# First modulation row summed by VectorE, and the lagged output matrices formed piecewise during the first projection

## The chip, the cores and the metric

The kernel runs on one core of a Trainium2 chip. The time is the device time of one execution, in microseconds (us). The kernel before takes 1801.37 us, the median of 3 runs (1799.45 to 1803.9). The profile comes from one further execution of 1798.16 us, whose span from its first to its last instruction is 1796.2 us.

## The reference, cut to what matters

The program is a stack of eleven phases over 256 tokens of width 1024: attention with compressed keys (mla), an MLP, a state-space mixer (s5), an MLP, and then gated feed-forward blocks with a recurrent block and a second attention between them. Everything is float32. The change touches only the first phase and what is prepared in it for later ones:

```python
cs = jax.nn.silu(c)                                   # (1, 1024)
shift, scale, gate = jnp.split(cs @ mod_mix_w[0] + mod_mix_b[0], 3, axis=-1)
h = x * (1.0 + scale) + shift                         # input of the first mixer
z = h @ w_in                                          # 448 columns: the first projection
cq = rms_norm(z[..., :256]); ckv = rms_norm(z[..., 256:384]); k_pe = rope(z[..., 384:])
q, kv = cq @ w_qb, ckv @ w_kvb                        # then causal attention over 8 heads
...
# s5, two phases later: y = C x, with C given as c_re, c_im (64 groups of 16 x 64)
# the kernel steps two tokens at a time and so also needs C times the decay ("lagged" matrices)
```

`mod_mix_w[0]` is 1024 x 3072; its first third gives the shift, the second the scale. The remaining thirds of the first two modulations (gate, and the shift and scale of the MLP behind) are needed only after the attention.

## The kernel before, in words

Each engine has its own instruction queue, written out by hand, and waits on named counters. Weights are streamed in chunks: SyncE (SP) issues `line(c)`, which loads chunk c of 1 MB into one of five `raw` slots; ScalarE (ACT) rounds it to a high part in `hi(c)`; VectorE (DVE) forms the remainder in `lo(c)`; TensorE (PE) multiplies with three products a tile. `line(c)` waits until the chunk that held its slot has been used.

The start. SP issues eight transfers of 1 MB, n = 0 to 7 (L590), two row blocks of one third each: n = 0 to 3 are the shift, 4 to 7 the scale. They go into four buffers `m0`, so that n = 4 to 7 each wait until PE has used the piece four places ahead (`m0_used`). PE multiplies each piece with the broadcast `csB` (L1157). Behind n = 5 SP issues chunk 0 of w_in, behind n = 6 the input x, and after n = 7, without any wait, chunks 1 and 2, two norm rows, two modulation pieces (L492) and chunks 3 and 4. ACT meanwhile issues its own transfers: three short ones, `b_re` and `b_im` of s5 (L1659, each 128 partitions x 32 runs of 64 bytes, 4096 pieces) and 16 small ones for `c_re` and `c_im` (L1665, 128 runs of 256 bytes each). Only after the last of them does ACT form the rotation table (L1382), copy the transposed decay parameters (L1669), round chunk 0, and, once GpSimd (POOL) has reduced the angles (POOL from L2344, counter `s5p_pool` at 2), form their exponentials and sines. DVE waits for the same counter for a reciprocal (L2274) and then builds h (L2282, L2283). PE transposes h (L714) and projects it in four passes `z_pass`.

Between the first projection and the attention. DVE normalises and rotates z (L1977 to L1982), forms the remainders for PE, and then `output_lag`, six operations on 128 x 1024 that turn the output matrices into the lagged ones (L2035 to L2040). It stands behind four transposes of c by PE (`s5_turn`, L948) and four copies by ACT (`s5_matrix`). POOL waits for it (`s5_lag`), stores the result, forms the input matrices (L2390 to L2394) and clears `wide_row` (L2410); ACT waits for that clearing in step 1 of the attention (`same_step`, L1410).

The modulation pieces. A later third is summed by DVE from four pieces of 1 MB, `piece(n)`: two scalar_tensor_tensor operations on 128 x 1024 (L1829, L1830). SP loads them with `fetch(n)` (L492) into two buffers, so `fetch(n)` waits for `piece(n - 2)`. Pieces 0 and 1 stand ahead of the two rotations of q, pieces 2 to 9 at the end of steps 0 to 3, 5, 6, 8 and 9 of the attention, chunk remainders `lo(6)` and `lo(7)` in steps 4 and 7, and pieces 10 and 11 behind. In SP's queue, 13 loads of short vectors (`cols`, L532, element by element) stand between `fetch(7)` and `fetch(8)`.

A step i of the attention on DVE: scale and mask the scores of head i (L2070, L2071) and take their maxima (L2074), normalise head i - 1 (L2080 to L2082), then from step 3 on form the remainder `hlo` of the output of head i - 3 (L1720), and then the piece. PE starts the output projection when the last `hlo` is there.

## Time and profile before

| | |
|---|---|
| median of 3 runs | 1801.37 us |
| profiled execution | 1798.16 us, span 1796.2 us |
| busy in the span | PE 92%, DVE 63%, ACT 46%, POOL 8% |
| busy in the first 200 us | PE 153.01, DVE 127.31, ACT 74.40, POOL 50.99 us |
| chain that ended last | PE 70%, DVE 16%, ACT 5% of the span |
| mean granted TensorE clock | 0.959 |

The page shows PE full from about 200 us on. Everything that the change touches lies ahead of that, in a stretch where PE has gaps. There the chain of waits runs through other engines and through transfers, and the busy shares of the page say little. The queues q1 and q10 are those of the transfers that SP and ACT issue; a "packet" is one contiguous piece of a transfer.

### The profile page before, as it was taken

The numbers are of one execution on the slowest core, as the hardware profiler recorded it, in microseconds if no ns is written. First come the engines' busy times: TensorE is split into PE (matmuls) and PEld (weight loads), VectorE is DVE, ScalarE is ACT, GpSimd is POOL, SyncE is SP. The second block draws the span as 40 slices with busy tenths as digits, with TensorE's granted clock in tenths as the row PEclk, the third lists the DMA queues.
The fourth block names the chain that finished last, engine by engine and source line by source line (L and its number), as shares of the span: only waits on it lengthen the run. The fifth ranks groups of instructions, "written<-read, shape, count | busy, mean of one in ns | idle before, by whom it ended". The sixth has DMA issues, their size and how long they took to land.

```text
span 1796.2 us, 20549 instructions
## 1 busy us (share of the span) xinstructions
PE 1660.3 (92%) x8247; PEld 1339.6 (75%) x8247; DVE 1139.6 (63%) x1346; ACT 835.0 (46%) x1129; POOL 150.2 (8%) x293
## 2 busy tenths in 40 slices
PE   8777899987989899999999859999999999799998
PEld 3645688865668688878888747888888888678887
DVE  1786867796989856485556757454655456655454
ACT  2443455544225455553434775433644444654443
POOL 4230010006621010000000000000000000000000
PEclk9877999997999899999999979999999999899999
DMA  9658468873029376546654625555546555236552
GB/s 301 237 177 236 164 219 314 290 255 118 1 78 335 127 246 246 171 139 206 223 188 164 223 70 188 187 188 188 182 157 217 182 194 191 96 99 215 183 192 85
DMA packets 165497, 335.45 MB, mean 187 GB/s; under 512 B 38773, under 2 KB 54462, under 8 KB 164251
## 3 DMA queue, kind: packets, MB, share of 16 engines
q1 hardware_dynamic: 144602, 292.63, 48.3%
q0 software_dynamic: 9696, 37.29, 5.7%
q10 hardware_dynamic: 11104, 4.23, 0.9%
q8 instruction: 65, 1.06, 0.2%
q14 instruction: 30, 0.24, 0.0%
HBM read 328.86 MB, written 6.83 MB: 187 GB/s over the span
## 4 chain that ended last, share of the span: by engine, by line
PE 70%; DVE 16%; ACT 5%; issue 3%; DMA 2%; POOL 2%; SPq 1%; DVEq 0%; ACTq 0%; POOLq 0%
PE ps L635 22%; PE ps L637 21%; PE ps L636 21%; DVE wlo L1715 2%; PE ps L720 2%; ACT whi L1186 1%; PE ps L1157 1%; SPq L532 1%; DVE xlo L1720 1%; PE ps L714 1%; DMA raw<-in_mlp_w 1%; DVE G L1829 1%; DMA work<-in_mod_mix_w 1%; DVE G L1830 1%; DVE work L2150 1%
## 5 line engine op out<-in xcount | busy, mean ns | idle before, releaser
L1715 DVE TENSOR_TENSOR wlo<-raw,whi 128x2048 fp32r<-128x2048 f32 (+2 forms) x247 | 559.5, 2285 | 267.4 <-ACT whi L1186 267.1
L1186 ACT ACTIVATE whi<-raw 128x2048 fp32r<-128x2048 f32 (+2 forms) x247 | 466.5, 1907 | 230.8 <-PE ps L637 185.8
L635 PE MATMUL ps<-whi,xhi 128*128 128x512 f32 (+2 forms) x1244 | 478.9, 385 | 21.4 <-DVE xlo L1720 21.4
L637 PE MATMUL ps<-whi,xlo 128*128 128x512 f32 (+2 forms) x1244 | 473.3, 380 | 0.0
L636 PE MATMUL ps<-wlo,xhi 128*128 128x512 f32 (+2 forms) x1244 | 473.2, 380 | 0.0
L635 PE MATMUL ps<-whi,hhi 128*128 128x512 f32 x736 | 295.0, 401 | 27.5 <-DVE hlo L1720 27.0
L637 PE MATMUL ps<-whi,hlo 128*128 128x512 f32 x736 | 289.3, 393 | 0.0
L636 PE MATMUL ps<-wlo,hhi 128*128 128x512 f32 x736 | 289.1, 393 | 0.0
L635 PEld LDWEIGHTS ps<-whi,xhi 128*128 128x128 f32 x1244 | 236.3, 190 | 66.9 <-DVE xlo L1720 25.0
L637 PEld LDWEIGHTS ps<-whi,xlo 128*128 128x128 f32 x1244 | 236.5, 190 | 44.3
L636 PEld LDWEIGHTS ps<-wlo,xhi 128*128 128x128 f32 x1244 | 236.6, 190 | 42.1
L635 PEld LDWEIGHTS ps<-whi,hhi 128*128 128x128 f32 x736 | 140.1, 190 | 62.3 <-DVE hlo L1720 31.2
L636 PEld LDWEIGHTS ps<-wlo,hhi 128*128 128x128 f32 x736 | 140.1, 190 | 30.3 <-issue 1.9
L637 PEld LDWEIGHTS ps<-whi,hlo 128*128 128x128 f32 x736 | 139.7, 190 | 29.9
L1720 DVE TENSOR_TENSOR hlo<-ps,hhi 128x512 fp32r<-128x512 f32 (+1 forms) x64 | 35.6, 588 | 152.0 <-ACT hhi L1352 137.5
L1352 ACT ACTIVATE hhi<-ps 128x512 fp32r<-128x512 f32 (+1 forms) x48 | 24.4, 560 | 186.5 <-PE ps L720 186.5
L1934 DVE SCALAR_TENSOR_TENSOR work<-ps,small,work 128x512 f32<-128x512 f32 (+1 forms) x48 | 33.7, 705 | 56.2 <-PE ps L637 51.7
L1192 ACT ACTIVATE xhi<-ps 128x512 fp32r<-128x512 f32 x44 | 25.2, 597 | 78.4 <-PE ps L714 78.4
L1307 ACT ACTIVATE work<-ps,small 128x128 f32<-128x128 f32 x128 | 36.3, 366 | 40.2 <-PE ps L720 40.2
L1347 ACT ACTIVATE work<-ps,small 128x512 f32<-128x512 f32 (+1 forms) x48 | 31.1, 654 | 44.0 <-PE ps L637 44.0
L635 PE MATMUL ps<-xhi,whi 128*128 128x256 f32 x120 | 36.7, 305 | 12.5 <-DVE xlo L1720 7.4
L720 PE MATMUL ps<-ident,work 128*128 128x128 f32 x320 | 42.8, 276 | 3.9 <-ACT work L1273 3.9
(347 smaller groups left out, 1602.6 us busy)
## 6 DMA issues: line engine op xcount, KB each, us to landing
raw<-in_mlp_w SPq DMA_DIRECT2D x64, 1024.0 KB, 5.3
raw<-in_ffn_w_gate SPq DMA_DIRECT2D x44, 1024.0 KB, 5.1
raw<-in_ffn_w_up SPq DMA_DIRECT2D x44, 1024.0 KB, 5.1
raw<-in_ffn_w_down SPq DMA_DIRECT2D x44, 1024.0 KB, 4.9
mod<-in_mod_ffn_w POOLq DMA_DIRECT2D x16, 1024.0 KB, 6.3
mod<-in_mod_mix_w POOLq DMA_DIRECT2D x12, 1024.0 KB, 6.3
work<-in_mod_mix_w SPq DMA_DIRECT2D x8, 1024.0 KB, 8.6
operands<-in_mod_ffn_w SPq DMA_DIRECT2D x8, 1024.0 KB, 8.1
```

Of the source, the lines that this page charges most:

```text
L635: pe.matmul(o, lh, rh, start=start, stop=False)
L636: pe.matmul(o, lh, rl, start=False, stop=False)
L637: return pe.matmul(o, ll, rh, start=False, stop=stop)
L720: last = pe.transpose(ps[:, bank, j * P:(j + 1) * P], src[:, j * P:(j + 1) * P], ident[:, :])
L1186: act.activation(whi[:, c % SPL, 0:n], raw[:, c % RAW, 0:n], ACT.Copy).then_inc(hi_done, 1)
L1192: act.activation(xhi[:, 4 * hf:4 * hf + 4, cols_of(tt)], ps[:, x_bank(tt, hf), :].rearrange("p (k n) -> p k n", k=4), ACT.Copy).then_inc(x ...
L1307: steps.did(act.activation(r[:, j * P:(j + 1) * P], ps[:, 4 + 2 * (i % 2) + tt, j * P:(j + 1) * P], ACT.Relu, bias=b1c[:, n:n + 1]))
L1347: act.activation(TMP[:, 512 * tt:512 * tt + lo], ps[:, 4 + tt, 0:lo], ACT.Silu, scale=x_scale(before, tt)).then_inc(act1, 1)
L1352: act.activation(hhi[:, 4 * (i % 2):4 * (i % 2) + n, cols_of(tt)], ps[:, 6 + tt, 0:n * P].rearrange("p (k n) -> p k n", k=n), ACT.Copy).th ...
L1715: dve.tensor_tensor(wlo[:, c % RAW, 0:n], raw[:, c % RAW, 0:n], whi[:, c % SPL, 0:n].bitcast(F32), ALU.subtract).then_inc(lo_done, 1)
L1720: return dve.tensor_tensor(dst, src, hi_part.bitcast(F32), ALU.subtract)
L1934: dve.scalar_tensor_tensor(TMP[:, 1024 + 512 * tt:1024 + 512 * tt + wide], up, rsq[:, 2 + tt:3 + tt], TMP[:, 512 * tt:512 * tt + wide], AL ...
```

## The change

- The shift is no longer summed by PE but by DVE, in the new `first_thirds`: eight operations on 128 x 1024 into `GA`, ahead of `lo(0)`. PE takes only the scale pieces and, at the end, sums `GA` over the partitions with two multiplications by ones.
- The transfers n = 0 to 7 alternate: even n are the shift, odd n the scale. n = 4 and 6 wait for DVE's sums (`m0_sum`), n = 5 and 7 for PE. x is issued behind n = 5, and chunk 0 behind n = 7.
- The bias rows of the first modulation go into `operands` rather than `GA` and `BA`.
- The transposes of c move ahead of the first projection pass on PE, their copies on ACT to between `hi(1)` and the second `x_hi`.
- `output_lag` is cut into five parts: two ahead of the second `x_lo`, one behind each token half's rotation, the last behind `lo(4)`.
- Pieces 0 and 1 move from the rotations into the attention; pieces 0 to 8 stand in steps 0 to 3, 5, 6, 8, 9 and 10, now ahead of `hlo`; pieces 9 to 11 behind.
- POOL copies the decay rows (L2341 before) after the first of three bias rows instead of after the third.

```diff
             for n in range(8):
-                third, kk = n // 4, n % 4
+                third, kk = n % 2, n // 2
                 if n >= 4:
-                    sp.wait_ge(m0_used, n - 3)
+                    sp.wait_ge(m0_used if third else m0_sum, kk - 1)
                 sp.dma_start(m0[n % 4], w0[:, 2 * kk:2 * kk + 2, D * third:D * (third + 1)]).then_inc(m0_in[n % 4], 16)
+                if n == 7:
+                    line(0)
                 if n == 5:
-                    line(0)
-                if n == 6:
                     sp.dma_start(X[:, :, :], ...).then_inc(x_in, 16)
...
             def mla():                                    # TensorE
                 turn("mla", 0)
+                pe.wait_ge(s5_in, 16 * 18)
+                pe.wait_ge(h_ready, 4)
+                for q in range(4):
+                    s5_turn(c_pad, q, q)
                 z_pass(0, 0)
...
-                pe.wait_ge(s5_in, 16 * 18)
-                for q, b in enumerate((1, 2, 3, 6)):
-                    s5_turn(c_pad, q, b)
+                pe.wait_ge(s5t_ok, 4)
...
-            for n in range(8):
-                third, kk = n // 4, n % 4
+            for kk in range(4):
+                n = 2 * kk + 1
...
-                if n == 4:
+                if kk == 1:
                     pe.wait_ge(s5a_in, 48)
                     pe.wait_ge(s5p_pool, 1)
...
+            pe.wait_ge(m0_sum, 4)
+            for hf in range(2):
+                pe.matmul(ps[:, hf, :], ones[:, :], GA[:, 512 * hf:512 * (hf + 1)], start=False, stop=True).then_inc(m0_done, 1)
...
+            def first_thirds():                           # VectorE
+                acc = GA[:, :]
+                for kk in range(4):
+                    n = 2 * kk
+                    dve.wait_ge(m0_in[n % 4], 16 * (n // 4 + 1))
+                    w = m0[n % 4]
+                    if kk == 0:
+                        do(dve.tensor_scalar(acc, w[:, 0, :], csil[:, 0:1], None, ALU.mult))
+                    else:
+                        dve.wait_ge(m0_sum, kk)
+                        do(dve.scalar_tensor_tensor(acc, w[:, 0, :], csil[:, n:n + 1], acc, ALU.mult, ALU.add))
+                    dve.scalar_tensor_tensor(acc, w[:, 1, :], csil[:, n + 1:n + 2], acc, ALU.mult, ALU.add).then_inc(m0_sum, 1)
...
                 lo(4)
+                output_lag(4)
...
-                piece(0)
                 for g in range(2):
-                    if g:
-                        piece(1)
...
+                    if n == 0:                            # in a step of the attention, ahead of hlo
+                        if i in (4, 7):
+                            lo(6 if i == 4 else 7)
+                        else:
+                            piece(i if i < 4 else i - 1 if i < 7 else i - 2)
                     if i >= 3:
...
-                    if n == 0:
-                        if i in (4, 7):
-                            lo(6 if i == 4 else 7)
-                        elif i < 10:
-                            piece(i + 2 if i < 4 else i + 1 if i < 7 else i)
...
+            first_thirds()
+            lo(0)
             dve.wait_ge(s5p_pool, S5P_ANGLE)
             dve.reciprocal(g0v[:, 8, :], g0v[:, 8, :]).then_inc(s5p_dve, 1)
-            lo(0)
```

SyncE's queue at the start, before: `in_mod_mix_w` are the pieces n, `in_mla_w_in` chunks 0 and 1, `in_mla_w_kvb` chunk 2.

```order
L590 DMA work<-in_mod_mix_w 128x2x1024 x6
L517 DMA raw<-in_mla_w_in 128x4x448
L590 DMA work<-in_mod_mix_w 128x2x1024
L594 DMA X<-in_x 128x2x1024
L590 DMA work<-in_mod_mix_w 128x2x1024
L517 DMA raw<-in_mla_w_in 128x4x448
L517 DMA raw<-in_mla_w_kvb 128x2048
```

The same place in the changed kernel.

```order
L592 DMA work<-in_mod_mix_w 128x2x1024 x6
L596 DMA X<-in_x 128x2x1024
L592 DMA work<-in_mod_mix_w 128x2x1024 x2
L519 DMA raw<-in_mla_w_in 128x4x448 x2
L519 DMA raw<-in_mla_w_kvb 128x2048
L599 DMA G<-in_mla_q_norm 128x256
```

Chunk 0 has moved behind the last piece, and x ahead of the last two.

VectorE's queue at the start, before: the rotation angles end with L2272; `G` holds the decay parameters, and L2282 begins h.

```order
L2272 TENSOR_SCALAR work<-work 128x64
L2274 RECIPROCAL G<-G 128x32
L1715 TENSOR_TENSOR wlo<-raw,whi 128x1792
L2282 SCALAR_TENSOR_TENSOR work<-ps,X 128x512
L2283 TENSOR_TENSOR work<-work,ps 128x512
```

The same place in the changed kernel.

```order
L2295 TENSOR_SCALAR work<-work 128x64
L1835 TENSOR_SCALAR GA<-work,small 128x1024
L1839 SCALAR_TENSOR_TENSOR GA<-work,small,GA 128x1024
L1838 SCALAR_TENSOR_TENSOR GA<-work,small,GA 128x1024
L1839 SCALAR_TENSOR_TENSOR GA<-work,small,GA 128x1024
L1838 SCALAR_TENSOR_TENSOR GA<-work,small,GA 128x1024
L1839 SCALAR_TENSOR_TENSOR GA<-work,small,GA 128x1024
L1838 SCALAR_TENSOR_TENSOR GA<-work,small,GA 128x1024
L1839 SCALAR_TENSOR_TENSOR GA<-work,small,GA 128x1024
L1720 TENSOR_TENSOR wlo<-raw,whi 128x1792
L2299 RECIPROCAL G<-G 128x32
L2306 SCALAR_TENSOR_TENSOR work<-ps,X 128x512
```

Eight operations were put in, and the remainder of chunk 0 now stands ahead of the reciprocal; h stands behind both, as before.

The end of the attention on VectorE, before: the last normalisation (step 8), and the last three `hlo`. The rows on `A` are pieces 8 to 11.

```order
L2082 TENSOR_SCALAR work<-work,small 128x256
L1720 TENSOR_TENSOR hlo<-ps,hhi 128x256
L1829 SCALAR_TENSOR_TENSOR A<-operands,small,A 128x1024
L1830 SCALAR_TENSOR_TENSOR A<-operands,small,A 128x1024
L1720 TENSOR_TENSOR hlo<-ps,hhi 128x256
L1829 SCALAR_TENSOR_TENSOR A<-operands,small,A 128x1024
L1830 SCALAR_TENSOR_TENSOR A<-operands,small,A 128x1024
L1720 TENSOR_TENSOR hlo<-ps,hhi 128x256
L1715 TENSOR_TENSOR wlo<-raw,whi 128x2048
```

The same place in the changed kernel; the rows on `B` are pieces 6 and 7.

```order
L2105 TENSOR_SCALAR work<-work,small 128x256
L1848 SCALAR_TENSOR_TENSOR B<-operands,small,B 128x1024
L1849 SCALAR_TENSOR_TENSOR B<-operands,small,B 128x1024
L1725 TENSOR_TENSOR hlo<-ps,hhi 128x256
L1848 SCALAR_TENSOR_TENSOR B<-operands,small,B 128x1024
L1849 SCALAR_TENSOR_TENSOR B<-operands,small,B 128x1024
L1725 TENSOR_TENSOR hlo<-ps,hhi 128x256
L1848 SCALAR_TENSOR_TENSOR A<-operands,small,A 128x1024
L1849 SCALAR_TENSOR_TENSOR A<-operands,small,A 128x1024
L1725 TENSOR_TENSOR hlo<-ps,hhi 128x256
L1720 TENSOR_TENSOR wlo<-raw,whi 128x2048
```

Pieces 6 to 8 stand ahead of the last `hlo` where pieces 8 and 9 stood, and three pieces rather than two remain behind it.

## Rows read from the trace of the kernel before

**Rows 1.** Timeline, 32 to 50 us: start, duration, operation, [idle before, releaser].
```profile
32.66 0.37 ACT L1669 ACTIVATE G<-ps 128x32 f32<-128x32 f32 x3 [3.42 <-PE ps L1166]
...
34.66 0.25 POOL L2344 TENSOR_TENSOR G<-G 128x32 f32<-128x32 f32 x1 [9.01 <-ACT G L1672]
...
38.71 0.35 DVE L2274 RECIPROCAL G<-G 128x32 f32<-128x32 f32 x1 [30.12 <-POOL G L2354]
...
42.78 0.69 DVE L2282 SCALAR_TENSOR_TENSOR work<-ps,X 128x512 f32<-128x512 f32 x1 [1.84 <-PE ps L1157]
...
49.38 0.74 PE L635 MATMUL ps<-whi,xhi 128*128 128x448 f32 x1 [2.83 <-DVE xlo L1720]
```

**Rows 2.** Timeline of SyncE's queue: start, duration, line, transfer.
```profile
18.62 3.80 SPq L590 DMA_DIRECT2D work<-in_mod_mix_w  x2
...
28.92 0.37 SPq L590 DMA_DIRECT2D work<-in_mod_mix_w  x1
```

**Rows 3.** Timeline of ScalarE and its queue (ACTq): start, duration, transfer or operation.
```profile
7.61 10.22 ACTq L1659 DMA_DIRECT2D mod<-in_ssm_b_im  x1
...
20.35 3.38 ACTq L1665 DMA_DIRECT2D mod<-in_ssm_c_re  x7
...
28.26 0.26 ACT L1382 ACTIVATE rope<-work 128x64 f32<-128x64 f32 x1 [20.09 <-issue]
```

**Rows 4.** Timeline of VectorE and TensorE, from 62 us to the attention.
```profile
62.45 1.91 PE L948 MATMUL ps<-ident,mod 128*128 128x128 f32 x16
...
82.31 2.21 DVE L1829 SCALAR_TENSOR_TENSOR G<-operands,small,G 128x1024 f32<-128x1024 f32 x1
...
86.81 0.28 PE L637 MATMUL ps<-whi,xlo 128*128 128x256 f32 x1
...
94.04 0.42 DVE L1977 TENSOR_TENSOR work<-ps,rope 128x256 f32<-128x256 f32 x1
...
97.78 1.11 PE L922 MATMUL ps<-ident,work 128*128 128x128 f32 x4 [6.59 <-DVE work L1982]
```

**Rows 5.** Timeline of VectorE, steps 0 and 3 of the attention.
```profile
104.42 0.28 DVE L2070 SCALAR_TENSOR_TENSOR work<-ps,mask 128x128 f32<-128x128 f32 x1
...
120.46 0.42 DVE L1720 TENSOR_TENSOR hlo<-ps,hhi 128x256 fp32r<-128x256 f32 x1 [1.11 <-ACT hhi L1467]
...
122.11 1.28 DVE L1830 SCALAR_TENSOR_TENSOR B<-operands,small,B 128x1024 f32<-128x1024 f32 x1
```

**Rows 6.** Timeline of SyncE's queue: first issue behind the short vectors.
```profile
143.39 0.87 SPq L492 DMA_DIRECT2D operands<-in_mod_ffn_w  x1
```

**Rows 7.** Timeline of VectorE and TensorE at the attention's end.
```profile
150.37 1.28 DVE L1829 SCALAR_TENSOR_TENSOR A<-operands,small,A 128x1024 f32<-128x1024 f32 x1 [2.58 <-DMA operands<-in_mod_ffn_w]
...
158.41 0.80 PE L635 MATMUL ps<-whi,hhi 128*128 128x512 f32 x1 [6.14 <-DVE hlo L1720]
```

**Rows 8.** DMA queues, 12 to 13 us: packets, MB, share of 16 engines.
```profile
q1 hardware_dynamic: 96, 0.39, 98.5%
q10 hardware_dynamic: 96, 0.01, 6.9%
```

**Rows 9.** DMA queues, 17 to 18 us (q1 has no row there).
```profile
q10 hardware_dynamic: 1573, 0.10, 108.0%
```

**Rows 10.** DMA queues, 0 to 17.2 us.
```profile
q10 hardware_dynamic: 3040, 0.22, 12.5%
```

**Rows 11.** DMA queues, 0 to 20.3 us.
```profile
q10 hardware_dynamic: 7227, 0.49, 24.1%
```

**Rows 12.** DMA queues, 20 to 55 us.
```profile
q1 hardware_dynamic: 3934, 11.99, 92.4%
```

**Rows 13.** DMA issues from 2.9 to 3.3 us: KB, us to landing (piece 0).
```profile
work<-in_mod_mix_w SPq DMA_DIRECT2D x1, 1024.0 KB, 5.7
```

**Rows 14.** Timeline of GpSimd: store of the lagged matrices, clearing of `wide_row`.
```profile
78.94 0.65 POOL L2403 DMA_DIRECT2D s_store<-mod  x1 [31.19 <-DVE mod L2040]
...
105.68 0.95 POOL L2410 MEMSET wide_row<- 128x1024 f32 x1
```

More of the change, by code:

```diff
@@ L237, in build_program @@
         brow = {"mlp0": mod[0:1, 6144:7168], "mlp1": wide_row[0:1, :], "lru": wide_row[0:1, :]}
+        mod_row = [operands[0:1, D * n:D * (n + 1)] for n in range(2)]
         csB = wide_row[:, :].rearrange("p (k n) -> p k n", k=KT)
@@ L1422, in mla @@
                     mean_root(2 * tt + 1, ssq[:, 2 * tt + 1:2 * tt + 2], 1 / KVL, eps_rms).then_inc(z_sq, 1)
-                for q, b in enumerate((1, 2, 3, 6)):
-                    s5_matrix(q, b)
                 hi(3)
@@ L1683, in _ @@
             hi(1)
+            for q in range(4):
+                s5_matrix(q, q)
             x_hi("mla", 1)
@@ L1998, in mla @@
                     dve.wait_ge(zn_ok, tt + 1)
+                    output_lag(2 + tt)
                 lo(3)
@@ L2022, in mla, with output_lag @@
                 lo(8)
+                piece(9)
                 piece(10)
                 piece(11)
-            def output_lag():
-                dve.wait_ge(s5t_ok, 4)
-                dve.wait_ge(s5p_pool, 3)
+            def output_lag(part):
                 wide = lambda k: g0v[:, k, :].rearrange("p (m i o) -> p m i o", i=4, o=1).to_broadcast([P, KT, 4, 32])
@@ L2034, in output_lag @@
                 tmp = H[:, 0, :].rearrange("p (m i c) -> p m i c", m=KT, i=4)
[L2035 to L2041 removed]
+                if part == 0:
+                    dve.wait_ge(s5t_ok, 4)
+                    dve.wait_ge(s5p_pool, 3)
+                    steps.did(dve.tensor_tensor(o_re, re, wide(3), ALU.mult))
+                    do(dve.tensor_tensor(o_im, im, wide(3), ALU.mult))
+                elif part == 1:
+                    do(dve.tensor_tensor(tmp, im, wide(10), ALU.mult))
+                elif part == 2:
+                    do(dve.tensor_tensor(o_re, o_re, tmp, ALU.add))
+                elif part == 3:
+                    do(dve.tensor_tensor(tmp, re, wide(10), ALU.mult))
+                else:
+                    dve.tensor_tensor(o_im, o_im, tmp, ALU.subtract).then_inc(s5_lag, 1)
+                    dve.wait_ge(s5_lag, 1)
             def decay():
@@ L2288, in _ @@
             lo(1)
+            output_lag(0)
+            output_lag(1)
             x_lo("mla", 1)
@@ L2334, in _ @@
                                pattern=[[-1, P]], channel_multiplier=1).then_inc(const_ok, 1)
-            for f in range(3):
-                open_third(f)
+            open_third(0)
             v = lambda k: g0v[:, k, :]
@@ L2342, in _ @@
                              ldt_rows.rearrange("q (g o) -> q g o", o=1).to_broadcast([PAIRS, 2, 64])).then_inc(s5p_pool, 1)
+            for f in (1, 2):
+                open_third(f)
             pool.wait_ge(s5p_act, 2)
```

27 lines of the change are left out of this document (9 added, 18 removed).

## The prediction

> **What bounds the kernel now.** I read the busy shares first: TensorE is full from some 200 us on, and the change touches nothing there. A change in the first 200 us therefore moves the end by what it moves the start of the first MLP. The timelines of the first 160 us, engine by engine, show three places that set this start.
>
> First, the start up to the first projection pass at 49.38 us [rows 1]. VectorE builds h from 42.78, when TensorE has the last piece. The pieces are late because n = 4 to 7 wait for TensorE: n = 4 is issued at 18.62, n = 7 at 28.92 [rows 2]. ScalarE is not late, but only just: its own transfers hold it until 28.26 [rows 3], and the angles, which VectorE needs ahead of h, are there at 38.7 [rows 1].
>
> Second, from the projection's end (62.45, call it Z [rows 4]) to the attention's first operation on VectorE (104.42 [rows 5]), 42 us. There the lagged matrices and two pieces stand ahead of the rotations, for the second of which TensorE waits 6.59 us [rows 4].
>
> Third, the attention's end. TensorE waits for the last `hlo` until 158.41; VectorE has waited there for pieces whose transfers SyncE issued only at 143.39 [rows 6, 7]. Between stand fetch(7) and the 13 short-vector loads, which could not begin before piece 5 was summed, at 123.39 [rows 5, 6]. So piece 5, then 20.0 us of SyncE's queue, then pieces 8 and 9 set the end of the attention.
>
> **The transfers at the start, which the trace shows to be the point.** Both issuing queues share the 16 DMA engines. While both have work they take turns packet by packet: 96 packets of 4 KB of q1 beside 96 of 64 bytes of q10 in one us [rows 8]. While q1 is empty, q10 alone moves 1573 in one us [rows 9]. Four pieces are 1,024 packets, 10.7 us at that rate, so q1 runs dry at about 16.1 us and stays so to 20.4 (n = 4 is issued at 18.62 [rows 2], its data follow 1.8 us later). In that hole nearly all of b_re and b_im goes through: 3040 packets by 17.2, 7227 by 20.3 [rows 10, 11].
>
> ScalarE cannot run ahead of this. It issues b_im from 7.61 to 17.83 [rows 3]. b_re and the three short loads are 4096 + 96 packets, of which 4192 - 3040 = 1152 were left at 17.2. The first c load is accepted at about 20.3, when 4192 + 4096 - 7227 = 1061 were left [rows 3, 11]. So, read from these two points, an issue is held until about 1,100 packets are left on q10. Behind these issues stand the rotation table and the whole chain of the decay.
>
> The Trainium skill ("DMA: Bandwidth & Descriptors", section "Queues, rings and completion order") says that an engine drains a whole packet, about 9 to 17 descriptors, from one row before it switches. If the 64-byte pieces went 9 to 17 at a turn, b_im would pass in a few us beside a full q1, ScalarE would not be held, and the sum would be that of rival 1. The equal counts (96 and 96) speak for one piece a turn here.
>
> **Term 1: when ScalarE is free.** n = 4 now waits for VectorE instead of TensorE. Piece 0 lands near 8.7 (5.7 after its issue [rows 13]); two operations of 128 x 1024 follow. The second is 1.28 us [rows 5]; the trace has no tensor_scalar of that size, and I bound it by 0 and by 2.2 (the slowest L1829 [rows 4]), and take 1.3, near the undisturbed row. n = 4 is then issued at about 11.4 (10.1 to 12.3), and its data join q1 before 16.1 at either end. It fills q1 until 18.8. n = 5 waits for TensorE's first piece, as n = 4 did, so it is issued at 18.6 and x and n = 6 right behind; data from 20.4. n = 7 comes at 22, and SyncE has no wait behind it. So the hole shrinks from 4.3 us to 1.6 us, and q1 is then full until its backlog ends.
>
> q10 gets some 900 packets through by 18.8 at 96 a us, and up to 3,200 in the hole. Thus b_re just ends, and b_im, held until 1,100 of b_re are left (near 19.9), is issued at about 20.4, when q1 is full again. The first c load needs 4096 - 1,100 = 3,000 of b_im gone, one for each packet of q1. q1 moved 3934 packets from 20 to 55 [rows 12]; without n = 4 (256) 3,680 remain, in 34.3 - 2.8 = 31.5 us, so until 51.7. 3,000 of them are through at 20.6 + 31.5 x 3,000 / 3,680 = 46.3. The last 512 (w_qb, 3 KB each) pass faster than the mean, so the 3,000th comes later; I take 47. The other 15 c loads took 7.9 us (20.35 to 28.26 [rows 3]); the first few still share with q1, which I put at 1.3 us more. ScalarE is free at 56.2 instead of 28.26: 28 us later.
>
> **Term 2: from there to the projection.** Rotation table 1.0 (four operations of 0.26 [rows 3]), copies, table load and exponential 2.0 (32.66 to 34.66), angles 4.05 (34.66 to 38.71) [rows 1]: VectorE is released at 63.3. Reciprocal, then h with its eight operations, 5.6 (eight of 0.69 [rows 1]): done at 69.2. All pieces, x and chunk 0 have then long landed, and the eight sums on VectorE (10 us) and TensorE's two extra multiplications are hidden in that wait; in rival 1, where this cover is gone, they still end before chunk 0 is there. The transposes of c now stand ahead of the first pass: 1.91 us for 16 [rows 4], 2.4 at the lower clock of a restart. First pass at 71.6 instead of 49.38: **+22.2 us** (17 to 30). Two parts of output_lag and their copies fall into the pass, hidden.
>
> **Term 3: projection to attention.** Gone: the six operations of output_lag in one block and ScalarE's copies for it, and pieces 0 and 1. Added: one part (1.28 by the row of its size [rows 5]) ahead of lo(3), one ahead of the copies of V. TensorE's second half of q waits for V: the block's 7.3 us go, but VectorE then waits for chunk 4's high part and pays one part, so I leave the end of q at Z + 24.4 (86.81 [rows 4]). The second rotation now follows at once, 3.7 us (94.04 to 97.73 [rows 4]), so TensorE has it at Z + 28.2 instead of 35.3: -7.1, and lo(5) behind it loses 0.4 of GpSimd's disturbance. Attention at Z + 34.5 instead of Z + 42: **-7.5** (-8.5 to -6).
>
> **Term 4: GpSimd.** It starts when the lagged matrices are there, at Z + 18.3 (behind lo(4)) instead of 16.5, and takes 27.7 us to the cleared wide_row (78.94 to 106.63 [rows 14]). So it ends at Z + 46, now 11.5 us into the attention; ScalarE waits for it in step 1, at 6 us. And pieces 0 and 1 run beside it, where such an operation took 2.21 instead of 1.28 [rows 4, 5]: four of them, 3.6 us. The two overlap: **+3.5** (+1 to +6).
>
> **Term 5: piece 5.** Before it ended 19.0 us after the attention's first operation (123.39 - 104.42 [rows 5]), being in step 3. Now it is in step 6. Steps last, by the same timeline, 3.8, 4.6, 4.6, then 4.9 with a piece and 4.5 with a remainder (6.0 and 5.6 before, less the wait of 1.11 for hhi [rows 5], which the piece now covers): 3.8 + 4.6 + 4.6 + 4.9 + 4.5 + 4.9 = 27.3, plus 4.8 in step 6: 32.1. **+13.1** (+11 to +14).
>
> **Term 6: after the short vectors.** The 20.0 us of SyncE's queue stay. Before, piece 9 too had to land ahead of the last hlo: 158.41 - 143.39 = 15.0 us. Now only piece 8: 7.0 (143.39 to 150.37 [rows 6, 7]) (5.3 if GpSimd's fetches no longer share), 2.6 for the piece, 0.4 for hlo: 9.2. **-5.8** (-6.7 to -5). Pieces 9 to 11 follow in 13 us, within the 18 us that TensorE needs before it asks for their sum, as before.
>
> Sum: 22.2 - 7.5 + 3.5 + 13.1 - 5.8 = +25.5 us. The profiled execution took 1798.16 us, giving 1823.7; the median of the runs lies 3.2 us above that execution, so about 1826 in their terms (1826.9; I round down, since terms 4 and 5 may overlap).
>
> **Rivals.**
> 1. ScalarE is not held, because an engine takes many small packets at a turn (at 9 or more, b_im is through in 5 us). Against it the equal counts [rows 8]. The chain of the pieces then counts: n = 7 at 22 instead of 28.92 [rows 2] and without chunk 0 ahead lands about 32, but chunk 0 lands at 35, and its remainder stands ahead of h: h at 38.7, first pass at 46.7, -2.7. Sum -2.7 - 7.5 + 3.5 + 13.1 - 5.8 = +0.6: 1802 (1796 to 1808). Chance 0.11. (It is the rule of the Trainium skill's "DMA: Bandwidth & Descriptors" quoted above.)
> 2. ScalarE is held, but the short vectors do not bind: the 20.0 us shrink, or piece 5 is not what starts them. Against it the issue at 143.39, 20.0 after piece 5 [rows 5, 6]. Terms 5 and 6 fall away, and the five waits of 1.11 (5.6) are won: 22.2 - 7.5 + 3.5 - 5.6 = +12.6: 1814. Chance 0.08.
> 3. Faster: the edits do what they move. Neither queue holds: -2.7 - 7.5 - 5.6 = -15.8: 1786. It needs the c loads through by 45 us and the short vectors elsewhere; the rows speak against both [rows 6, 8]. Chance 0.04.
> 4. Held longer: q10 gets less than one packet a turn, or the last c loads land late. If all of b_im waits for q1's end (51.7, by [rows 12]), ScalarE is free at 62 and the time is 1832 or more. Chance 0.07.
>
> **How the numbers follow.** The forecast has 0.70: its own range, from the bounds of its terms, is 1815 to 1836. With rival 2 and the near part of rival 4 that makes 8 in 10: 1808 to 1836. A measurement of this kernel can tell about 0.3% (5.4 us). Slower by more than that: 0.70 + 0.08 + 0.07 and a fifth of rival 1, 0.88. The same: most of rival 1, 0.08. Faster: 0.04.
>
> **What would show it.** Right: the issue of b_im ends near 20, the first c load is accepted near 47, the rotation table runs near 56, TensorE idles some 25 us ahead of the first pass near 71; the attention starts near 120, the short vectors near 155, the output projection near 184. q1 and q10 show equal counts from 21 to 45 us. Wrong: a rotation table before 35 us (then rival 1), or more than 200 packets a us on q10 beside a full q1; short vectors that start less than 25 us after the attention (rival 2).

## The result, and the profile after

The kernel after takes 1834.53 us (median of 4 runs, 1832.17 to 1837.3), the kernel before in the same session 1802.53 us (4 runs, 1799.45 to 1803.9): a ratio of 1.018 (95% interval 1.0158 to 1.0203), 32 us slower. Forecast were 1826 us, in a range of 1808 to 1836. The profiled execution of after took 1837.3 us, the highest of its four, that of before 1798.16, below the lowest of its four; between the two profiles the difference is 39.1 us. One profiled execution of the study, that of e4 below (1928.81 us at a granted clock of 0.825; its other eleven took 1799.01 to 1803.33), fell into a slower state of the chip and counts in no ratio.

Where it went is read at six marks of the two profiled executions (us):

| mark | before | after | later by |
|---|---|---|---|
| rotation table: ScalarE is past its transfers | 28.26 | 54.57 | 26.3 |
| first projection pass | 49.38 | 72.33 | 23.0 |
| attention starts on VectorE | 104.42 | 118.44 | 14.0 |
| second operation of piece 5 | 122.11 | 156.69 | 34.6 |
| output projection starts on TensorE | 158.41 | 194.70 | 36.3 |
| first layer norm (L1776, L1781 after) | 176.97 | 212.66 | 35.7 |

What is left of the execution behind the layer norm (its time less the mark) is 1621.2 us before and 1624.6 after; in the profiles of the experiments, e4 aside, it lies between 1621 and 1628, so the 3 us between the two kernels there are within what this stretch varies by.

The start, in the timeline of ScalarE's queue (start, duration, transfer or operation), to be laid beside [rows 3]:

```profile
7.67 12.73 ACTq L1662 DMA_DIRECT2D mod<-in_ssm_b_im  x1
20.43 29.76 ACTq L1668 DMA_DIRECT2D mod<-in_ssm_c_re  x8
...
54.57 0.26 ACT L1387 ACTIVATE rope<-work 128x64 f32<-128x64 f32 x1 [46.40 <-issue]
```

`[46.40 <-issue]` is the point: for 46 us ScalarE waits for nothing but its own issues. The chain of waits splits the second row: the first c load alone is held for 25.34 us. The DMA queues from 28 to 29 and from 33 to 34 us (packets, MB, share of 16 engines) show what holds it:

```profile
q1 hardware_dynamic: 94, 0.39, 95.6%
q10 hardware_dynamic: 95, 0.01, 6.7%
```

```profile
q1 hardware_dynamic: 190, 0.34, 95.7%
q10 hardware_dynamic: 191, 0.01, 13.7%
```

The equal counts of [rows 8] are there again, also where q1's packets are less than half as large (1,792 bytes) and so twice as many. TensorE's timeline shows the price, answering to the last row of [rows 1]:

```profile
65.07 2.35 PE L716 MATMUL ps<-ident,work 128*128 128x128 f32 x8 [23.49 <-DVE work L2307]
69.03 3.65 PE L951 MATMUL ps<-ident,mod 128*128 128x128 f32 x16 [1.62 <-DVE work L2307]
72.33 0.72 PE L637 MATMUL ps<-whi,xhi 128*128 128x448 f32 x1
```

The attention on VectorE (and two rows of ScalarE and TensorE that it waits for), answering to [rows 5]:

```profile
118.44 0.28 DVE L2093 SCALAR_TENSOR_TENSOR work<-ps,mask 128x128 f32<-128x128 f32 x1
...
119.61 2.24 DVE L1848 SCALAR_TENSOR_TENSOR G<-operands,small,G 128x1024 f32<-128x1024 f32 x1
```

```profile
130.77 2.23 ACT L1415 ACTIVATE wide_row<-ps 32x128 f32<-32x128 f32 x8 [4.38 <-POOL wide_row L2437]
```

```profile
138.58 0.29 DVE L2093 SCALAR_TENSOR_TENSOR work<-ps,mask 128x128 f32<-128x128 f32 x1 [3.23 <-PE ps L1002]
...
156.69 1.28 DVE L1849 SCALAR_TENSOR_TENSOR B<-operands,small,B 128x1024 f32<-128x1024 f32 x1
```

Pieces 0 and 1 take 2.2 us an operation (GpSimd is working beside them), and ahead of the fourth step VectorE waits for scores, since ScalarE waited 4.38 us for the clearing of `wide_row`. Then SyncE's queue, answering to [rows 6] and to the 20.0 us in front of it:

```profile
158.42 0.47 SPq L534 DMA_DIRECT2D small<-in_ssm_d  x1
...
159.55 8.05 SPq L534 DMA_DIRECT2D small<-in_mlp_b  x2
167.65 2.71 SPq L534 DMA_DIRECT2D small<-in_lru_b_in  x1
170.40 7.16 SPq L534 DMA_DIRECT2D small<-in_lru_conv_b  x1
177.61 3.12 SPq L534 DMA_DIRECT2D small<-in_lru_b_r  x1
...
185.14 14.62 SPq L494 DMA_DIRECT2D operands<-in_mod_ffn_w  x4
```

```profile
168.05 2.25 POOL L494 DMA_DIRECT2D mod<-in_mod_ffn_w  x3 [37.37 <-DMA s_store<-mod]
```

The 13 short vectors took 26.7 us here. Two of their loads are far longer than the same in the kernel before (`lru_conv_b` 1.77, `lru_b_r` 0.58 there), from the moment at which GpSimd issues three fetches of 1 MB. At the end of the attention (VectorE, TensorE), answering to [rows 7]:

```profile
191.58 1.28 DVE L1848 SCALAR_TENSOR_TENSOR A<-operands,small,A 128x1024 f32<-128x1024 f32 x1 [21.92 <-DMA operands<-in_mod_ffn_w]
```

```profile
194.70 0.80 PE L637 MATMUL ps<-whi,hhi 128*128 128x512 f32 x1 [24.93 <-DVE hlo L1725]
```

VectorE stands 21.92 us for piece 8, and TensorE with it.

### The profile page after: what moved, and what is told of

Same layout as the page of the kernel before. It is cut to its first block, busy times and chain, and to the rows that moved or that the text cites. A ratio compares the mean times of both kernels' runs of the same rounds, so it can differ in the third digit from the quotient of the medians.

```text
span 1835.2 us, 20511 instructions
## 1 busy us (share of the span) xinstructions
PE 1658.0 (90%) x8219; PEld 1337.6 (73%) x8219; DVE 1149.1 (63%) x1354; ACT 835.3 (46%) x1129; POOL 152.8 (8%) x293
## 4 chain that ended last, share of the span: by engine, by line
PE 68%; DVE 15%; ACT 5%; POOL 4%; issue 4%; ACTq 2%; SPq 1%; DMA 1%; DVEq 0%; POOLq 0%
PE ps L637 22%; PE ps L638 21%; PE ps L639 21%; DVE wlo L1720 2%; ACTq L1668 2%; PE ps L722 2%; SPq L534 1%; ACT whi L1191 1%; DVE work L2173 1%; POOL mod L2421 1%; PE ps L716 1%; DVE xlo L1725 1%; POOL mod L2455 1%; POOL mod L2347 1%; DVE small L1785 0%
## 5 line engine op out<-in xcount | busy, mean ns | idle before, releaser
L716 PE MATMUL ps<-ident,work 128*128 128x128 f32 x176 | 26.7, 288 | 32.5 <-DVE work L2307 23.5
L716 PEld LDWEIGHTS ps<-ident,work 128*128 128x128 f32 x176 | 20.0, 144 | 41.3 <-issue 30.2
```

The lines of the kernel that those rows point to most:

```text
L716: last = pe.transpose(ps[:, x_bank(tt, hf), j * P:(j + 1) * P], src[:, tt, k * P:(k + 1) * P], ident[:, :])
```

## The experiments

Twelve kernels. The times are medians of 4 to 12 executions; the marks (us) are those of one profiled execution, which for e2 is a slower one (1814.12 us, its median being 1806.45). The profile of after is the slowest of its four, so that a mark can be up to 1 us earlier in a run for no other reason: the first pass is at 71.3 to 71.7 in e3, e7, e8 and e10, whose edits do not touch it, and at 72.33 in after.

| run | median (us) | ratio to before | ScalarE free | first pass | attention | output projection | layer norm |
|---|---|---|---|---|---|---|---|
| e1 after, hole back | 1818.30 | 1.0081 (1.0066 to 1.0096) | 33.24 | 53.07 | 99.47 | 174.12 | 191.25 |
| e2 before, x early | 1806.45 | 1.0033 (1.0012 to 1.0055) | 43.97 | 59.28 | 113.92 | 167.73 | 186.61 |
| e3 after, vectors early | 1819.82 | 1.0089 (1.0073 to 1.0106) | 53.84 | 71.62 | 117.50 | 174.54 | 194.26 |
| e4 e1 and e3 together | 1801.22 | 0.9990 (0.9981 to 0.9999) | 33.08 | 53.03 | 99.64 | 155.74 | 176.82 |
| e5 before, vectors early | 1800.27 | 0.9984 (0.9974 to 0.9994) | 27.04 | 50.19 | 104.29 | 155.21 | 175.03 |
| e6 e5, piece first | 1793.98 | 0.9948 (0.9936 to 0.9961) | 27.50 | 50.53 | 106.05 | 150.66 | 170.29 |
| e7 after, pieces as before | 1821.46 | 1.0093 (1.0079 to 1.0107) | 53.81 | 71.33 | 126.42 | 179.05 | 196.92 |
| e8 after, GpSimd's fetches later | 1831.99 | 1.0153 (1.0139 to 1.0168) | 53.93 | 71.66 | 117.27 | 184.82 | 207.82 |
| e9 before, x and chunk 1 early | 1804.33 | 1.0024 (1.0002 to 1.0047) | 34.90 | 51.24 | 105.50 | 159.76 | 178.70 |
| e10 after, half of GpSimd's work | 1826.91 | 1.0141 (1.0121 to 1.0160) | 53.98 | 71.55 | 116.31 | 183.82 | 201.19 |
| e11 before, vectors at 80, piece first | 1795.20 | 0.9965 (0.9950 to 0.9979) | 28.30 | 49.98 | 104.22 | 148.18 | 168.70 |
| e12 before, queue full | 1826.80 | 1.0141 (1.0113 to 1.0169) | 57.85 | 73.15 | 128.63 | 180.85 | 200.43 |

(The marks of e4 agree with those of e1 up to the attention, as its edit wants it.)

### The start: e1, e2, e9, e12

Does the hole in SyncE's data queue, and it alone, decide when ScalarE is free? e1 gives it back to the kernel after, by one wait:

```diff
                 if n >= 4:
                     sp.wait_ge(m0_used if third else m0_sum, kk - 1)
+                if n == 4:
+                    sp.wait_ge(m0_used, 1)
```

> The kernel after, with one wait added: the fifth weight transfer (n = 4) also waits for TensorE's first use, as in the kernel before, so that SyncE's data queue runs dry again from about 16 to 20 us. Theory (the two queues take turns, ScalarE is held by its own queue): b_im's issue ends near 18 us, the first c load is accepted near 20, the rotation table runs near 28 instead of 54.6, the first projection pass is at 47 to 52 us instead of 72.7, and the time is 1811 us (1807 to 1816). Rival (the start is late by the change's own work: VectorE's sums, the transposes ahead of the pass): the hole does nothing, first pass near 72, time 1830 to 1837.

Measured: 1818.3 us, 16 less than after; ScalarE's queue and release:

```profile
7.63 9.81 ACTq L1664 DMA_DIRECT2D mod<-in_ssm_b_im  x1
17.47 6.09 ACTq L1670 DMA_DIRECT2D mod<-in_ssm_c_re  x8
23.59 9.61 ACTq L1670 DMA_DIRECT2D mod<-in_ssm_c_im  x8
33.24 0.26 ACT L1389 ACTIVATE rope<-work 128x64 f32<-128x64 f32 x1 [25.08 <-issue]
```

Most of the hold is gone (ScalarE is free at 33.24, 5.0 later than before), and the first pass is 19.3 us earlier than in after. The rival, the change's own work, is left with what e1 still lacks against before, 3.7 us: the transposes of c ahead of the pass, and chunk 0, which now lands behind all the pieces (VectorE waits for its high part until 42.10). The time fell by less than I expected (1811, and 1816 at most); half of the miss is that the first pass came back by 19.3 and not by 23. The rest is in part the profile of after, a slow one for its kernel: profile against profile, e1 is 19.0 us faster, median against median 16.2.

e2 does the opposite in the kernel before: x is issued behind the fourth weight transfer, nothing else.

```diff
             for n in range(8):
+                if n == 4:
+                    sp.dma_start(X[:, :, :], ...)
                 if n >= 4:
                     sp.wait_ge(m0_used, n - 3)
...
-                if n == 6:
-                    sp.dma_start(X[:, :, :], ...)
```

> The kernel before, with one transfer moved: x (1 MB) is issued right behind the fourth weight transfer instead of behind the seventh, which fills 2.7 of the 4.3 us in which SyncE's data queue was dry. Nothing of the change is in it. Theory: ScalarE is held by its own queue, the first c load is accepted near 47 us instead of 20.35, the rotation table runs near 55, the first pass is near 69 instead of 49.4, and the time is 1802.5 + 20 = 1822 us (1816 to 1828). Rival (the queues' turns do not matter; the change's own work made the start late): first pass at 49, time 1800 to 1805.

A miss. Measured: b_im's issue ended at 20.1, as in after (20.4), but ScalarE was free at 43.97, not 55, and the median is only 3.4 us above that of before beside it, with a wide spread (1801.66 to 1821.0). The DMA queues from 24 to 25 us show why:

```profile
q10 hardware_dynamic: 1850, 0.12, 127.6%
q1 hardware_dynamic: 18, 0.07, 34.7%
```

SyncE's queue ran dry a second time, since n = 6 waits for TensorE until 24.91. e9 puts chunk 1 in front of that wait as well:

```diff
                 if n == 5:
                     line(0)
+                    line(1)
...
-            line(1)
```

> The kernel before, with x issued right behind the fourth weight transfer, and chunk 1 right behind chunk 0 ahead of n = 6. In the run that moved x alone, SyncE's data queue ran dry a second time, at 23 to 25 us, because n = 6 waits for TensorE until 24.9 us, and 2,900 small packets of ScalarE's queue went through there: ScalarE was free at 44.0. Theory: with that hole shut too, ScalarE is held as in the kernel after, the rotation table runs at 52 to 56 us, the first pass is near 69 instead of 49.4, and the time is 1803 + 20 = 1823 us (1818 to 1828). Rival (the length of the hold is set by something else in the kernel after): ScalarE free near 44 again, time 1806 to 1814.

A miss again, 1804.33 us: n = 5 itself was issued late, near 22.5, chunks 0 and 1 behind it, and the second hole was wider than in e2:

```profile
q10 hardware_dynamic: 2237, 0.14, 155.4%
...
q1 hardware_dynamic: 1, 0.00, 0.1%
```

(again 24 to 25 us). ScalarE was free at 34.9. The edit did not shut the hole that it was meant to shut, and what it did fits the theory: more dry time, less hold. e12 leaves no dry time, all three transfers standing ahead of every wait:

```diff
+                if n == 4:
+                    sp.dma_start(X[:, :, :], ...)
+                    line(0)
+                    line(1)
                 if n >= 4:
                     sp.wait_ge(m0_used, n - 3)
```

> The kernel before, with x, chunk 0 and chunk 1 all issued right behind the fourth weight transfer, ahead of every wait: 2.8 MB that keep SyncE's data queue full from 5 us until n = 4 to 7 follow. In the two runs that moved less, the queue still ran dry at 23 to 25 us, behind n = 5. Theory: with no dry stretch at all ScalarE's small packets get one turn for each packet of the other queue, near 96 a us; b_im's issue ends near 37 us instead of 17.8, and the first c load is accepted only near the other queue's end, 50 to 54 us. ScalarE is free at 57 to 62 us instead of 28.3, the first pass is at 72 to 78 instead of 49.4, and the time is 1803 + 26 = 1829 us (1820 to 1835). Rival (the hold has another cause, or small packets find their way beside a full queue): ScalarE free by 45 us, time under 1815.

Measured 1826.8 us. ScalarE's queue and release, then TensorE's last pieces, VectorE's release ahead of h, and TensorE's first pass:

```profile
7.73 27.98 ACTq L1658 DMA_DIRECT2D mod<-in_ssm_b_im  x1
35.74 18.21 ACTq L1664 DMA_DIRECT2D mod<-in_ssm_c_re  x8
53.98 3.82 ACTq L1664 DMA_DIRECT2D mod<-in_ssm_c_im  x8
57.85 0.26 ACT L1381 ACTIVATE rope<-work 128x64 f32<-128x64 f32 x1 [49.68 <-issue]
```

```profile
32.85 10.57 PE L1156 MATMUL ps<-work,wide_row 128*128 128x512 f32 x24
```

```profile
64.74 0.35 DVE L2273 RECIPROCAL G<-G 128x32 f32<-128x32 f32 x1 [56.15 <-POOL G L2353]
```

```profile
73.15 0.74 PE L634 MATMUL ps<-whi,xhi 128*128 128x448 f32 x1 [2.37 <-DVE xlo L1719]
```

Three transfers issued earlier, and nothing else of the change, make the kernel before 25.5 us slower. The pieces are not what is late in it: TensorE has summed them at 43.4, while VectorE waits for the angles until 64.74. That is shown, then: ScalarE's hold follows the time in which the data queue of the other engine is dry, in both kernels and in both directions. Counted in the traces' records of single packets, q1 is empty between 16 and 26 us for 3.7 us in before, 3.8 in e1, 1.8 in e9, 1.6 in e2, 0.9 in after and not at all in e12; ScalarE is free at 28.3, 33.2, 34.9, 44.0, 54.6 and 57.9. The dry time is not all of it, as the first two show: from 23 to 25 us q10 moves 767 packets in before, beside a q1 that is busy for two thirds, and 117 in e1, where q1 is full.

The spread of e2 and e9 (up to 22 us between executions of one kernel) stays open. The 43.97 us of e2 belong to one of its slower executions, 7.7 us above its median; the profile of e9 (1805.54) lies near its median.

### The end of the attention: e3, e4, e8

e3 moves the short vectors of the kernel after, nothing else:

```diff
             line(7)
+            for dst, src in ((dskip, ...), ..., (lru_conv ...)):
+                cols(dst, src, small2_in)
             fetch(sp, 2)
...
             for n in range(4, 8):
                 fetch(sp, n)
-            for dst, src in (...):
-                cols(dst, src, small2_in)
             for n in range(8, 12):
                 fetch(sp, n)
```

> The kernel after, with the 13 short-vector loads moved from between fetch(7) and fetch(8) to ahead of fetch(2), where SyncE's queue is idle (99.9 to 124.1 us). Theory (the short vectors bind the end of the attention: VectorE waits 21.9 us for piece 8): fetch(8) follows piece 6, near 166; piece 8 is summed near 173 instead of 191.6; the output projection starts near 176 instead of 194.7, and the time is 1834.5 - 18 = 1816 us (1812 to 1822). Rival (the wait is only the first of several: pieces 9 to 11 or the rows of the sum come late next): the output projection starts early but what follows it waits, time 1825 to 1834.

Measured 1819.82 us, 14.7 less. The output projection starts at 174.54 as expected, 20.2 earlier, the layer norm 18.4 earlier. Piece 8 on VectorE:

```profile
171.42 1.28 DVE L1848 SCALAR_TENSOR_TENSOR A<-operands,small,A 128x1024 f32<-128x1024 f32 x1 [1.86 <-DMA operands<-in_mod_ffn_w]
```

The wait of 21.92 us was the short vectors'. At their new place, with no fetch beside them, they took 18.7 us (99.17 to 117.83).

> Both edits together on the kernel after: n = 4 waits for TensorE's first use, and the short vectors go ahead of fetch(2). If the two terms are independent, the gains add: 1834.5 - 23 - 18 = 1793 us (1788 to 1800), some 9 us faster than the kernel before. Rival (the stages share a limit, for instance chunk loads or pieces that come late once the start is early): the sum falls short, 1800 to 1812.

Measured 1801.22 us: not 1793. The two gains add as they were measured (16.2 and 14.7, so 1803.6), and the expectation had both too large (23 and 18). The layer norm shows a small shortfall as well: the output projection is 18.4 earlier than in e1, the layer norm 14.4. Pieces 9, 10 and 11 now wait 2.62, 2.55 and 0.48 us for their transfers, and ahead of the layer norm VectorE waits for a weight chunk that SyncE issues only behind them, at 163.55, and ScalarE rounds at 172.59. So the change as it stands, freed of its two collisions, is as fast as the kernel before to within 0.2%, and not the 9 us faster that I expected.

e8 asks what made the short vectors 26.7 us long, by one wait on GpSimd:

```diff
+            pool.wait_ge(piece_used, 9)
             for n in range(12, 15):
                 fetch(pool, n)
```

> The kernel after, with one wait added: GpSimd's three fetches (pieces 12 to 14, 168.05 us) wait until piece 8 is summed, so they no longer fall among SyncE's short vectors. Theory (the short vectors took 26.7 us instead of 20.0 because those fetches' packets took turns with theirs: conv_b 7.16 and b_r 3.12 us of issue instead of 1.77 and 0.58): the 13 loads take 19.5 to 20.5 us, fetch(8) is issued near 178.5, time 1834.5 - 7 = 1827.5 us (1825 to 1831). Rival (ScalarE's store of s, or the loads themselves, make them slow): conv_b stays near 7 us, time 1832 to 1837.

SyncE's queue in e8:

```profile
157.27 0.47 SPq L534 DMA_DIRECT2D small<-in_ssm_d  x1
...
169.15 1.23 SPq L534 DMA_DIRECT2D small<-in_lru_conv_b  x1
170.41 0.85 SPq L534 DMA_DIRECT2D small<-in_lru_b_r  x1
...
175.97 13.90 SPq L494 DMA_DIRECT2D operands<-in_mod_ffn_w  x4
```

18.7 us: what made them slow is shown. The time is 1831.99, outside the 1825 to 1831 that I expected, and its 2.5 us less than after are no more than the executions of either kernel differ by. The trace has the rest: GpSimd's fetches now share with pieces 9 to 11, piece 11 waits 7.09 us, and of the 9.9 us that the output projection is earlier (1.2 of them are there at the attention's start already) 4.8 are left at the layer norm.

### GpSimd and the place of the pieces: e10, e7

e10 leaves out `input_matrices(bl_dg, 5, 7)` of GpSimd (a part of the computation), with one tiny operation in its place for the counter.

> The kernel after, with one part of the computation left out: GpSimd's second set of input matrices (bl_dg, 13.6 us of its work), so that wide_row is cleared near 115 us instead of 130.7. Theory (terms 4 and 5 came out 4 us larger than forecast because pieces 0 and 1 beside GpSimd and the wait for wide_row add up instead of overlapping): the four operations of pieces 0 and 1 take 1.28 us instead of 2.2, the attention does not wait before its fourth step (3.23 us), piece 5 ends near 151 instead of 158, and as the short vectors then bind the time is 1834.5 - 7 = 1827.5 us (1824 to 1831). Rival (the wait for wide_row overlaps with work that is needed anyway): piece 5 ends 3 to 4 us earlier, time 1830 to 1834.

VectorE in e10, attention's start, piece 0, and piece 5's first operation:

```profile
116.31 0.28 DVE L2093 SCALAR_TENSOR_TENSOR work<-ps,mask 128x128 f32<-128x128 f32 x1
...
117.49 1.28 DVE L1848 SCALAR_TENSOR_TENSOR G<-operands,small,G 128x1024 f32<-128x1024 f32 x1
...
146.12 1.28 DVE L1848 SCALAR_TENSOR_TENSOR B<-operands,small,B 128x1024 f32<-128x1024 f32 x1
```

Every operation of a piece is 1.28 us, no wait stands ahead of the fourth step, and from the attention's start to the end of piece 5 it is 32.4 us (148.7 - 116.3) instead of 39.5. The time is 7.6 us lower, as expected; 2.1 us of that stand at the attention's start already (116.31 against 118.44). The Trainium skill ("GPSIMD Engine Reference", section "1. Specifications") says that GpSimd's SBUF interfaces are shared with VectorE and that instructions of VectorE with two SBUF inputs contend for them. The trace agrees: 2.24 and 1.28 us are such an instruction with and without GpSimd at work.

e7 puts pieces 0 and 1 back ahead of the two rotations, and 2 to 9 into the attention:

```diff
+                piece(0)
                 for g in range(2):
+                    if g:
+                        piece(1)
                     dve.wait_ge(pe_pass, passed(3 + g))
...
-                piece(9)
                 piece(10)
...
-                            piece(i if i < 4 else i - 1 if i < 7 else i - 2)
+                            piece(i + 2 if i < 4 else i + 1 if i < 7 else i)
```

> The kernel after, with pieces 0 and 1 back where they stood (ahead of the two rotations of q) and pieces 2 to 9 in the attention; the order piece-then-remainder, the start and the split of the lagged matrices stay. Theory (terms 3 to 6: the place of the pieces moves piece 5, which starts the short vectors): attention starts near 124 us instead of 118.4, no wait for wide_row in it, piece 5 ends near 143.5 instead of 158, fetch(8) is issued near 163.5 instead of 185, ln_glue near 197 instead of 212.7, time 1834.5 - 16 = 1818 us (1813 to 1823). Rival (the pieces' place is a wash, the delay of the start carries everything): 1830 to 1837.

Measured 1821.46 us, 13 less. The attention starts 8 us later (126.42) and still the output projection starts 15.6 us earlier, since piece 5 ends at 144.0, and fetch(8) is issued at 163.8. GpSimd's fetches (167.59) come behind the short vectors again, which took 19.4 us. Of the change's middle part, then, the move of the pieces is what cost; the split of the lagged matrices without it won nothing: from the projection's end (82.2) to the attention it is 44.2 us in e7 against 42.0 before.

### A faster version: e5, e6, e11

Two things stood out. The short vectors bind the kernel before too, and in the attention's steps a piece ahead of the remainder hides the five waits of 1.11 us for ScalarE [rows 5], the one part of the change that is shown to help by itself. e5 is the kernel before with the short vectors between chunks 4 and 5; e6 has the other order too:

```diff
+                    if n == 0:
+                        if i in (4, 7):
+                            lo(6 if i == 4 else 7)
+                        elif i < 10:
+                            piece(i + 2 if i < 4 else i + 1 if i < 7 else i)
                     if i >= 3:
                         ...
                         rest(hlo[:, h, :], ...).then_inc(o_ok, 1)
-                    if n == 0:
-                        ...
```

> The kernel before, with the 13 short-vector loads moved from between fetch(7) and fetch(8) to between chunks 4 and 5, where SyncE's queue is idle (42 to 60 us). Theory (they set the end of the attention also there, but only by the two waits for pieces 8 and 9, 2.58 + 1.86 us): the last hlo comes 4.4 us earlier, time 1803 - 4.4 = 1798.6 us (1796 to 1801). Rival (they bind nothing before, since the next pieces are as late by their own transfers): 1802 to 1804.

> The same as the run with the early short vectors on the kernel before, and in each step of the attention the piece now stands ahead of the remainder (hlo), which is a part of the change. Theory: the five waits of 1.11 us for ScalarE's hhi go (5.6 us), so 1798.6 - 5.6 = 1793 us (1790 to 1797), faster than both kernels. Rival (a transfer takes the place of the wait: pieces alternate between two buffers, some 5 us each): 1797 to 1801.

Measured 1800.27 us (2.7 less than the 1802.93 of before beside it) and 1793.98 us (9.0 less, ratio 0.9948). Both lie in their expected ranges, e5 nearer to its upper end; e6 is 0.5% faster than before, beyond its interval, and so faster than both kernels. In e5 and e6 chunk 5 is late, so e11 puts the short vectors ahead of fetch(2) instead:

> The kernel before, with the piece ahead of the remainder in the attention's steps, and the short vectors ahead of fetch(2) (78 to 98 us) instead of between chunks 4 and 5, where chunk 5 was issued at 70.9 instead of 60.2 us and the attention started 1.7 us late. Theory: chunk 5 and the attention's start are again where they were, fetch(2) is issued near 98 and its piece still lands ahead of step 0's place for it, time 1794 - 1.7 = 1792 us (1789 to 1795). Rival (fetch(2) to fetch(5), now 10 us later, are late for their steps): 1794 to 1800.

Measured 1795.2 us, ratio 0.9965, just outside what I expected (1789 to 1795) and in the rival's range; it can't be told from e6 (the intervals overlap). The attention did start where it used to (104.22), and the layer norm is 1.6 us earlier than in e6, but VectorE waits 5.54 us for piece 11, and the median shows nothing of the gain. Which of the two places of the short vectors is better stays open.

## Why the prediction was right, point by point

Forecast +25.5 us (1826), measured +32 in the medians: the direction, the place and the mechanism were right, and the time lies in the range. That it lies there is in part luck. Terms 4 and 6 came out beyond their own bounds, and the +36.3 of the profiles at the output projection would be 1838 in the prediction's terms (1798.16 + 36.3 + 3.2), above its 1836; the medians differ by 4 us less. (The upper bounds of the five terms add up to +39, 1840, and not to the 1836 that is given for them.) At the output projection, in the profiles, the terms are:

| term | forecast | measured | from |
|---|---|---|---|
| 1 ScalarE free later (part of 2) | +28 | +26.3 | 54.57 - 28.26 |
| 2 and its effect on the end of the projection | +22.2 | +21.2 | 83.6 - 62.45 |
| 3 projection to attention | -7.5 | -7.1 | 34.8 instead of 42.0 |
| 4 GpSimd | +3.5 | +7.1 | 39.5 - 32.4 (e10) |
| 5 piece 5 later in the attention | +13.1 | +13.4 | 32.4 - 19.0 |
| 6 after the short vectors | -5.8 | +1.7 | 36.7 instead of 35.0 |
| sum of 2 to 6 | +25.5 | +36.3 | 194.70 - 158.41 |

Terms 1 and 2. The issue of b_im ended at 20.4, the first c load was accepted at 45.8 (forecast 47), the first pass ran at 72.33 (71.6). e1 and e12 show that the hold is this term and what sets it. The holes were both shorter than I had worked out, 3.7 and 0.9 us where I had 4.3 and 1.6. And the 0.7 us by which the first pass missed hide three misses: ScalarE was free 1.6 earlier than forecast, from there to VectorE's release (63.31) it took 8.7 instead of 7.1, and the transposes of c held the first pass for 3.3 (69.03 to 72.33) instead of 2.4. The passes themselves ran faster than before (0.36 instead of 0.57 us for the early ones), which gives back 1.8 of the 23.0 us: TensorE was granted 0.50 of its clock from 49.4 to 54 us before and 0.84 from 72.3 to 75.3 after, with the transposes of c in front; in e12, without them, it was 0.50 again.

The step between them that doesn't hold is a small one: "an issue is held until about 1,100 packets are left on q10". At 4192 packets up to b_re's end and 8288 up to b_im's, the counts at the acceptance give 900 and 1290 left in after, but 360 and 16 in e12. The first of the two points from which I had read it was itself misread: I counted at 17.2 us, but b_im's issue ended at 17.83 (7.61 + 10.22 [rows 3]), when q10 had moved 4119 packets and 73 of the 4192 were left. So the kernel before alone had 73 and 1061, and no fixed number. It cost some 1 us here, since in after the two counts happened to lie near 1,100: luck.

Term 3 stands as forecast, by the wrong share: with the split alone the stretch is 44.2 us (e7), 2.2 longer than before, and the move of the two pieces takes it to 34.8.

Term 4 is mis-sized, 7.1 instead of 3.5 (its own range ended at 6). I let the slower pieces (3.6 us) and the wait for `wide_row` overlap. They add, because behind the clearing (130.7) stand another 7.9 us until VectorE has the scores of step 3 (138.58): ScalarE's eight copies and TensorE's transposes and scores, which I had not counted. So VectorE, though 3.6 us late, still waits 3.23.

Term 5 is confirmed by e10 to 0.3 us.

Term 6 is the largest miss, and has the wrong sign: "The 20.0 us of SyncE's queue stay". They became 27.2 (157.97 to 185.14), and 9.56 us came behind them instead of 9.2. (The 9.2 is not the sum that stands beside it, 7.0 + 2.6 + 0.4 = 10.0; it is the middle between that and 8.3, with 5.3 for the transfer.) The 20.0 were read from a stretch in which no other queue had work: GpSimd's three fetches came at 155.31 there, 12 us behind the short vectors. They wait for ScalarE's store, at 145.07 before and 162.40 after, 17 us later, while the short vectors moved by 34.6. So the two streams, which had passed one after the other, met. It is the mechanism of term 1 over again, on other queues, and I did not look for it a second time. e8 shows it.

Of the rivals, the first (ScalarE not held, 1802) is excluded by ScalarE's release at 54.57, where it asked for one before 35. The rule of the Trainium skill on which it rests ("DMA: Bandwidth & Descriptors", section "Queues, rings and completion order") would have an engine drain some 9 to 17 descriptors of one row before it switches. The prediction took the equal counts of a microsecond to speak against that, but turns of nine pieces on both queues would give equal counts too, and ScalarE would be held all the same; rival 1 needed long turns of the small pieces alone. The records of single packets decide the length of a turn. In the kernel before, from 11.5 to 15 us, a 64-byte piece starts within the last 4 ns of 286 of 315 pieces of 4 KB (in 4 ns that lie 40 to 120 ns earlier it is 75 to 108 of them, as chance has it with 16 engines at work); in after, from 27 to 31 us, it is 338 of 364. So the two queues changed places piece by piece here, and by the measurement the rule does not hold for them. The second (short vectors don't bind, 1814) is excluded by e3. The third asked for neither to hold; e4, in which both are nearly lifted (ScalarE is free at 33.08), is the nearest to it and gives 1801 and not 1786. The fourth (held longer, 1832 or more) gave about the time that was measured, but not by its reason: ScalarE was free 1.6 us earlier than forecast. What the sum lacked, 11 us at the mark of the output projection, is in terms 4 and 6.

## What to carry to other kernels

A queue of large transfers that never runs dry is not free: small transfers on another queue live from its gaps (96 packets in a microsecond beside it, 1573 without it [rows 8, 9]), and the engine that issues them stands until they are through, with all that is queued behind. Before closing a gap, look at what went through it; and when a stage moves, lay every transfer stream that moved by another amount beside it again, since two that never met may meet. Work moved off a chain has to be followed to what it releases (here the next fetch), not to where it fits.

## What was not expected of the hardware

- The hold is very sharp in the dry time: 2.8 us less of it moved ScalarE's release from 28 to 54 us (before, after), and 9 us of release lie between the profiles of e2 and e9, whose dry times differ by 0.2 us (1.6 and 1.8). How much of these 9 us is the edit and how much the execution is not shown.
- An issue's release isn't a fixed backlog of its queue: 1290, 1061, 900, 360, 73 and 16 packets were left at six such points (after, before and e12). What decides it stays open.
- Loads of short vectors, element by element, are slowed also by GpSimd's queue: 7.16 instead of 1.23 us for one issue beside three transfers of 1 MB.
- A tensor_scalar of 128 x 1024 took 0.75 us, where the scalar_tensor_tensor of that size takes 1.28; the prediction had bounded it by 0 and 2.2 and taken 1.3.
